# Two 64-wide heads per TensorE turn, or one: unpairing the half-array matmuls of two attention stages

## The reference

```python
def causal_mla_attention(q_nope, q_rope, k_nope, k_rope, v):   # 8 heads, q and k 64+32 wide, v 64 wide
    sc = einsum('bqhd,bkhd->bhqk', qn, k_nope) + einsum('bqhr,bkr->bhqk', qr, k_rope)
    sc = where(mask, sc * scale, -inf)
    p = softmax(sc, axis=-1)
    return einsum('bhqk,bkhd->bqhd', p, v)

def mixer_b(q, k, v, rel_bias):          # groups with (window, dilation) (128,1), (512,4), (2048,16)
    for g, (window, dilation) in enumerate(DIL_PAIRS):
        o, l = dilated_group(...)         # banded softmax with a bias by relative distance
    wts = softmax(stack(lses), axis=0)
    return sum(wts[..., None] * stack(outs), axis=0)
```

## Time and profile before

| | us |
|---|---|
| median of 3 runs | 1055.5 (1055.49 to 1056.89) |
| profiled execution | 1055.49 |
| its span in the trace | 1053.5 |
| TensorE busy | 1012.3 (96%) |
| VectorE busy | 700.0 (66%) |
| ScalarE busy | 536.9 (51%) |
| granted TensorE clock, mean | 0.993 |

### The profile page before, as it was taken

One profiled execution on the slowest core, in us unless ns is written; L12 is line 12 of the kernel. 1 busy time (PEld: TensorE's weight loads), 2 busy tenths in 40 slices (PEclk: granted clock), 3 DMA queues, 4 the chain that ended last, 5 costly groups with the idle time before them and its releaser, 6 DMA issues.

```text
span 1053.5 us, 19826 instructions
## 1 busy us (share of the span) xinstructions
PE 1012.3 (96%) x8502; PEld 983.1 (93%) x8502; DVE 700.0 (66%) x1213; ACT 536.9 (51%) x903; POOL 39.0 (4%) x75
## 2 busy tenths in 40 slices
PE   5999999999988999999999999999999999999995
PEld 3899999988987899999999999999999999999985
DVE  3478787556687577776756679655557765555485
ACT  4453444455555655544444477654455554445453
POOL 5000000010000001000000000004000000000000
PEclk8999999999999999999999999999999999999998
DMA  9979899875735346487573656436256575565511
GB/s 306 379 261 317 292 339 316 292 265 190 220 93 187 126 155 181 162 278 241 199 237 130 194 161 200 155 113 187 68 170 223 178 240 167 193 196 165 200 41 40
DMA packets 144463, 212.27 MB, mean 201 GB/s; under 512 B 4259, under 2 KB 121239, under 8 KB 144376
## 3 DMA queue, kind: packets, MB, share of 16 engines
q1 hardware_dynamic: 138928, 194.40, 55.6%
q0 software_dynamic: 5184, 16.30, 4.8%
q10 hardware_dynamic: 264, 0.31, 0.1%
HBM read 209.88 MB, written 1.11 MB: 200 GB/s over the span
## 4 chain that ended last, share of the span: by engine, by line
PE 63%; issue 22%; DVE 8%; DMA 3%; ACT 3%; SPq 0%; POOL 0%; POOLq 0%; DVEq 0%; ACTq 0%
PE PS L460 61%; DVE wlo L1774 4%; DMA SC<-in_w_ada_dram 3%; PE PS L468 1%; ACT whi L1291 1%; DVE SC L1732 1%; ACT SC L1278 1%; DVE xT L1741 0%; ACT SC L1283 0%; DVE SC L2207 0%; DVE W L1732 0%; DVE hl L1741 0%; DVE SC L1738 0%; DVE SC L1741 0%; DVE st L1744 0%
## 5 line engine op out<-in xcount | busy, mean ns | idle before, releaser
L1774 DVE TENSOR_TENSOR wlo<-raw,whi 128x1024 fp32r<-128x1024 f32 (+2 forms) x331 | 386.4, 1186 | 197.7 <-ACT whi L1291 197.3
L1291 ACT ACTIVATE whi<-raw 128x1024 fp32r<-128x1024 f32 (+2 forms) x331 | 331.5, 1022 | 173.9 <-PE PS L460 132.9
L460 PE MATMUL PS<-hh,whi 128*128 128x256 f32 (+1 forms) x1376 | 393.6, 286 | 8.0 <-DVE wlo L1774 5.8
L460 PE MATMUL PS<-hh,wlo 128*128 128x256 f32 (+1 forms) x1376 | 388.7, 282 | 0.0
L460 PE MATMUL PS<-hl,whi 128*128 128x256 f32 (+1 forms) x1376 | 387.8, 282 | 0.0
L460 PE MATMUL PS<-SR,whi 128*128 128x256 f32 (+1 forms) x1824 | 329.0, 283 | 3.9 <-DVE wlo L1774 1.4
L460 PEld LDWEIGHTS PS<-SR,whi 128*128 128x128 f32 x1824 | 279.8, 188 | 8.8 <-issue 3.1
L460 PEld LDWEIGHTS PS<-hh,whi 128*128 128x128 f32 x1376 | 260.3, 189 | 12.3 <-DVE wlo L1774 7.0
L460 PEld LDWEIGHTS PS<-hl,whi 128*128 128x128 f32 x1376 | 261.1, 190 | 0.4
L460 PEld LDWEIGHTS PS<-hh,wlo 128*128 128x128 f32 x1376 | 260.7, 189 | 0.0
L460 PE MATMUL PS<-SR,wlo 128*128 128x256 f32 (+1 forms) x912 | 256.6, 281 | 0.0
(11 more groups left out here) (183 smaller groups left out, 722.0 us busy)
## 6 DMA issues: line engine op xcount, KB each, us to landing
raw<-in_ffn_w_dram SPq DMA_DIRECT2D x60, 1024.0 KB, 7.2
raw<-in_w_in_dram SPq DMA_DIRECT2D x38, 1024.0 KB, 5.5
raw<-in_w_ff_dram SPq DMA_DIRECT2D x32, 1024.0 KB, 5.3
raw<-in_w_ada_dram SPq DMA_DIRECT2D x16, 1024.0 KB, 6.7
SC<-in_w_ada_dram POOLq DMA_DIRECT2D x12, 1024.0 KB, 5.7
SC<-in_w_ada_dram SPq DMA_DIRECT2D x8, 1024.0 KB, 12.3
raw<-in_w_out_dram SPq DMA_DIRECT2D x8, 1024.0 KB, 4.8
raw<-in_ffn_w_dram SPq DMA_DIRECT2D x8, 768.0 KB, 12.9
```

Source lines behind the costliest of these rows:

```text
L460: return e.matmul(o, l, r, start=start, stop=stop, skip_group_check=True)
L1291: e.activation(hi_part(p), raw_part(p), ACT.Copy).then_inc(*hi_done.up(p.i))
L1774: e.tensor_tensor(lo_part(p), raw_part(p), hi32(hi_part(p)), ALU.subtract).then_inc(*lo_done.up(p.i))
```

## The change

`values1`, `scores_b` and `values_b` take one head or unit at a time instead of two. The loops call them in every iteration: `values1(i - 3)` from i = 3, `scores_b(i)` for i below 8, `values_b(i - 2)` from i = 2. Each signals by itself, and each waits only for what it reads. In branch B the order of the units changes from (both heads of one T) to (both T of one head), and with it the addresses that the bias loads read; their sizes, number and buffers stay. The products are the same, and so is their number.

```diff
-            def values1(k):
-                b = (7, 3)[k % 2]
-                on.wait_ge(act_done, ("pt1", 2 * k), ("pt1", 2 * k + 1))
...
-                for j, (at, src) in enumerate(((0, slice(0, 256)), (128, slice(256, 384)))):
-                    for h in (2 * k, 2 * k + 1):
-                        po = 64 * (h % 2)
-                        m = mm(PS[po:po + 64, b, at:256], v_sb[:, j, 64 * h:64 * h + 64], pt1[h % 3][:, src], j == 0, j == 1)
-                m.then_inc(*count(("v1", 2 * k), ("v1", 2 * k + 1)))
+            def values1(h):
+                k, b = h // 2, (7, 3)[h // 2 % 2]
+                po, pt = 64 * (h % 2), pt1[h % 3]
+                on.wait_ge(act_done, ("pt1", h))
...
+                mm(PS[po:po + 64, b, 0:256], v_sb[:, 0, 64 * h:64 * h + 64], pt[:, 0:256], True, False)
+                mm(PS[po:po + 64, b, 128:256], v_sb[:, 1, 64 * h:64 * h + 64], pt[:, 256:384], False, True).then_inc(*count(("v1", h)))
...
-                if i >= 4 and i % 2 == 0:
-                    values1(i // 2 - 2)
+                if i >= 3:
+                    values1(i - 3)
...
-            def scores_b(n):
-                f0, T = n // 2, n % 2
-                on.wait_ge(*((act_done, ("s_a", 6), ("s_a", 7)) if n == 0 else (dve_done, ("s_b", 2 * n - 2), ("s_b", 2 * n - 1))))
...
-                    for half in range(2):
-                        at = slice(64 * half, 64 * half + 64)
-                        m = mm(PS[:, 4 + half, o:o + w], qbT[at, f, 128 * T:128 * T + 128], kbT[at, f, ks])
-                m.then_inc(*count(("s_b", 2 * n), ("s_b", 2 * n + 1)))
+            def scores_b(u):
+                s, T = u // 2, u % 2
+                b, po = 4 + u % 2, 64 * (s % 2)
+                on.wait_ge(*((act_done, ("s_a", 6 + u)) if u < 2 else (dve_done, ("s_b", u - 2))))
...
+                    m = mm(PS[:, b, o:o + n], qbT[po:po + 64, f, 128 * T:128 * T + 128], kbT[po:po + 64, f, ks])
+                m.then_inc(*count(("s_b", u)))
...
-            def values_b(n):
-                f, T = n // 2, n % 2
-                on.wait_ge(act_done, ("pt2", 8 + 2 * n), ("pt2", 9 + 2 * n), ("back2", 6), ("back2", 7), ("back2", 8))
...
-                for j in range(4):
-                    for half in range(2):
-                        s = 2 * f + half
...
-                m.then_inc(*count(("v_b", 2 * n), ("v_b", 2 * n + 1)))
+            def values_b(u):
+                s, T = u // 2, u % 2
+                po = 64 * (s % 2)
+                on.wait_ge(act_done, ("pt2", 8 + u), ("back2", 6), ("back2", 7), ("back2", 8))
...
+                for j, (blk, hd) in enumerate(((0, s), (1, s), (T, 4 + s), (T, 8 + s))):
+                    m = mm(PS[po:po + 64, 7, 128 * T:128 * T + 128], vb[:, blk, 64 * hd:64 * hd + 64], pt2[u % 2][:, 128 * j:128 * j + 128], j == 0, j == 3)
+                m.then_inc(*count(("v_b", u)))
 
             for i in range(10):
-                if i < 8 and i % 2 == 0:
-                    scores_b(i // 2)
+                if i < 8:
+                    scores_b(i)
                 behind2(1)
                 if 1 <= i <= 8:
                     turn2("b", i - 1, False)
-                if i >= 3 and i % 2:
-                    values_b((i - 3) // 2)
+                if i >= 2:
+                    values_b(i - 2)
...
             for u in range(8):
-                s, T, half = 2 * (u // 4) + u % 2, u // 2 % 2, u % 2
+                s, T = u // 2, u % 2
```

More of the change, by code:

```diff
@@ L798, in turn1 @@
                 m.then_inc(*count(("pt1", h)))
-            def values1(k):
-                b = (7, 3)[k % 2]
-                on.wait_ge(act_done, ("pt1", 2 * k), ("pt1", 2 * k + 1))
[L803 to L808, removed]
-                for j, (at, src) in enumerate(((0, slice(0, 256)), (128, slice(256, 384)))):
-                    for h in (2 * k, 2 * k + 1):
-                        po = 64 * (h % 2)
-                        m = mm(PS[po:po + 64, b, at:256], v_sb[:, j, 64 * h:64 * h + 64], pt1[h % 3][:, src], j == 0, j == 1)
-                m.then_inc(*count(("v1", 2 * k), ("v1", 2 * k + 1)))
+            def values1(h):
+                k, b = h // 2, (7, 3)[h // 2 % 2]
+                po, pt = 64 * (h % 2), pt1[h % 3]
+                on.wait_ge(act_done, ("pt1", h))
+                if h % 2 == 0:
+                    if k == 0:
+                        on.wait_ge(act_done, ("qkT", 1, 1))
+                    elif k == 1:
+                        on.wait_ge(*back1_free(6))
+                    else:
+                        on.wait_ge(dve_done, ("oa", k - 2))
+                mm(PS[po:po + 64, b, 0:256], v_sb[:, 0, 64 * h:64 * h + 64], pt[:, 0:256], True, False)
+                mm(PS[po:po + 64, b, 128:256], v_sb[:, 1, 64 * h:64 * h + 64], pt[:, 256:384], False, True).then_inc(*count(("v1", h)))
             for i in range(HEADS + 3):
@@ L1033, in pe_program @@
             behind2(2)
-            def scores_b(n):
-                f0, T = n // 2, n % 2
-                on.wait_ge(*((act_done, ("s_a", 6), ("s_a", 7)) if n == 0 else (dve_done, ("s_b", 2 * n - 2), ("s_b", 2 * n - 1))))
-                for g, (o, w) in enumerate(((0, 256), (256, 128), (384, 128))):
-                    f = 2 * g + f0
+            def scores_b(u):
+                s, T = u // 2, u % 2
+                b, po = 4 + u % 2, 64 * (s % 2)
+                on.wait_ge(*((act_done, ("s_a", 6 + u)) if u < 2 else (dve_done, ("s_b", u - 2))))
+                for g, (o, n) in enumerate(((0, 256), (256, 128), (384, 128))):
+                    f = 2 * g + s // 2
@@ L1040, in scores_b @@
                     on.wait_ge(dve_done, ("back2", f // 2), ("back2", 3 + f // 2))
                     ks = slice(0, 256) if g == 0 else slice(128 * T, 128 * T + 128)
-                    for half in range(2):
-                        at = slice(64 * half, 64 * half + 64)
-                        m = mm(PS[:, 4 + half, o:o + w], qbT[at, f, 128 * T:128 * T + 128], kbT[at, f, ks])
-                m.then_inc(*count(("s_b", 2 * n), ("s_b", 2 * n + 1)))
-            def values_b(n):
-                f, T = n // 2, n % 2
-                on.wait_ge(act_done, ("pt2", 8 + 2 * n), ("pt2", 9 + 2 * n), ("back2", 6), ("back2", 7), ("back2", 8))
-                if n == 0:
+                    m = mm(PS[:, b, o:o + n], qbT[po:po + 64, f, 128 * T:128 * T + 128], kbT[po:po + 64, f, ks])
@@ L1051, in values_b @@
+                m.then_inc(*count(("s_b", u)))
[3 more added lines that the diff above has]
+                on.wait_ge(act_done, ("pt2", 8 + u), ("back2", 6), ("back2", 7), ("back2", 8))
+                if u == 0:
                     on.wait_ge(dve_done, ("oA", 7))
-                if n == 2:
+                if u == 4:
                     on.wait_ge(dve_done, ("oB", 0))
-                for j in range(4):
-                    for half in range(2):
-                        s = 2 * f + half
-                        blk, hd = ((0, s), (1, s), (T, 4 + s), (T, 8 + s))[j]
-                        m = mm(PS[64 * half:64 * half + 64, 7, 128 * T:128 * T + 128], vb[:, blk, 64 * hd:64 * hd + 64],
-                               pt2[half][:, 128 * j:128 * j + 128], j == 0, j == 3)
@@ L1263, in pool_program @@
                     src = bass.AP(scratch.tensor, base, [[1, 128], [255, n], [1, 128]])
-                    e.dma_start(bias_at[half][:, o:o + 128 * n].rearrange("p (c k) -> p c k", k=128), src).then_inc(*bias_in[half].landed(u))
+                    e.dma_start(bias_at[T][:, o:o + 128 * n].rearrange("p (c k) -> p c k", k=128), src).then_inc(*bias_in[T].landed(u))
             on.wait_ge(dve_done, ("gm", 3, 7))
@@ L2393, in dve_program @@
                 if i < 8:
-                    c, half, p = st[:, 160 + 8 * (i % 4):168 + 8 * (i % 4)], i % 2, p2[(8 + i) % 3]
+                    c, T, p = st[:, 160 + 8 * (i % 4):168 + 8 * (i % 4)], i % 2, p2[(8 + i) % 3]
                     lo_for(("s_b", i))
-                    on.wait_ge(bias_in[half], i)
+                    on.wait_ge(bias_in[T], i)
                     on.wait_ge(mm_done, ("s_b", i), ("pt2", 5 + i))
@@ L2399, in dve_program @@
                         on.wait_ge(dve_done, ("p2", "b", i - 4))
-                    e.tensor_tensor_reduce(p, PS[:, 4 + i % 2, :], bias_at[half], -1.0, 3.0e38, ALU.add, ALU.min,
+                    e.tensor_tensor_reduce(p, PS[:, 4 + i % 2, :], bias_at[T], -1.0, 3.0e38, ALU.add, ALU.min,
                                            accum_out=c[:, 0:1]).then_inc(*dve_done.up(("s_b", i)))
```

## The result

| | before | after |
|---|---|---|
| median, us | 1055.95 (4 runs, 1055.49 to 1056.89) | 1066.16 (4 runs, 1064.69 to 1067.33) |
| profiled execution, its span, us | 1055.49, 1053.5 | 1066.5, 1064.5 |
| granted clock, mean | 0.993 | 0.989 |

The account below looks back on a forecast made before the run. TensorE was taken to bound branch B fully, and the first block only beyond its waits for VectorE and ScalarE. Branch B 7.8 plus first block 1.3 made 9.1 us on 1055.49: 1064.6 us, range 1061.0 to 1068.0.

Parts of the forecast that it names:

- A lone unit costs a pair's time: Attention groups: paired halves share one 0.109 us slot, so a lone unit takes as many slots as a pair.
- Rival A: Both stages: half an array takes half a slot, 0.055 us; only entries and exits cost, +1.2 us; chance 0.07.
- Rival C: Branch B: lone units show their weight loads, about +4 us more, 1068.8 us; chance 0.05.
- The number of new groups: Branch B: one scores group, three of values and scores, one of values are new, 9.4 us in sum.
- The wait of 1.6 us goes: End of branch B: fewer ScalarE pieces ahead of the last transposes' copy, so TensorE's 1.6 us wait ahead of last values disappears.
- Branch B +7.8: Branch B: new groups cost 9.4 us with nothing to hide them, less the 1.6 us wait.
- First block: First block's attention: four new `values1` groups, 4.0 us in all, partly taken up by three waits; 1.3 us remain.
- 0.81 in iteration 6, and 0.2 is left: First block's attention: the second new 1.0 us group meets a 0.81 us wait, leaving TensorE 0.2 us late.
- Rival B: Waits only move: first block pays all 4.0 us, branch B's 1.6 stays, 1068.9 us; chance 0.10 including half of it.
- Nothing vanishes behind the stages: Behind both attention stages: hardly a wait is left, so the whole 9.1 us delay reaches the end.
- The total: Whole kernel: 9.1 us on 1055.49 us gives 1064.6 us, 0.9% slower.
- the ends of these waits don't move: First block's attention: ScalarE and VectorE are the chain and keep their order, so TensorE's waits end when they did.

Follow-up runs that it names:

- e2: Only `scores_b` unpaired, units in the old order, against the kernel before; ratio 1.0058.
- e3: Only `values_b` unpaired, units in the old order, against the kernel before; ratio 1.0031.
- e5: Kernel before, pairs kept, with the last piece ahead of ScalarE's last `pt2` copy in branch B moved behind it; ratio 0.9994.
- e8: Kernel after, with the last piece put ahead of ScalarE's last `pt2` copy in branch B again; 1067.05 us in one execution.
- e6: e5, plus ScalarE doing its pieces one step earlier in the first block's attention; 1050.21 us, ratio 0.993 against the kernel before.
- e1: Only `values1` and its call unpaired, branch B as in the kernel before; ratio 1.0007, 1057.59 us.
- e10: e6 with the unpaired `values1` of after; ratio 0.9956 against the kernel before.
- e4: Kernel before, pairs in one group, but all matmuls of one half ahead of the other's in all three pair groups; ratio 1.0034.
- e9: Kernel before, `values_b` alone with halves alternating in blocks of three, three, one and one matmuls; 1058.22 us in one execution.
- e7: Kernel before, halves alternating in blocks of two matmuls in all three pair groups; 1057.97 us in one execution.

## Why the prediction was right

- **A lone unit costs a pair's time: right.** 8 records in 1.09 us, starts 0.11 us apart but for the first pause of 0.16, groups of 2.84 us for 2.86. Rival A needed gaps of 0.055 and is refuted. Rival C needed gaps of 0.14 to 0.19, and is refuted by the same rows. The Trainium skill (TensorE: Matmul & The Clock Gate, Part 3), from which C came, ties the overlap of weight loads to different row groups; the lone groups load the same tile record after record and hide loads of 0.136 and 0.186 us all the same, so the measurement decides against that rule here. The same part also lets a load run ahead into a background weight buffer; no run here shows whether that is what happens.
- **The number of new groups: right.** The parts are 5.0 + 3.1 us in e2 and e3, 7.57 in after.
- **The wait of 1.6 us goes because unit 6's key is noted one iteration earlier: right,** shown by e5 and e8 from both sides.
- **Branch B +7.8: right**, with 7.57. The wait that went was worth 1.7 (e5, e8) rather than the 1.6 shown.
- **First block: the mechanism was right, the size 0.3 too large.** 0.98 us for 1.3. The step that failed is "0.81 in iteration 6, and 0.2 is left" and the like: it set groups of 1.0 us against the waits as shown, and each wait is worth 0.16 more (e6). So iteration 4 takes 0.99 of 1.31 + 0.16 and leaves 0.48, shown as 0.33; iteration 6 takes 0.97 and leaves TensorE late by nothing, iteration 8 likewise with 1.03. Only the fourth group, 0.99, is left, and 0.98 was measured. e1 repeats it, and e10 shows four full prices without cover. Rival B, waits that only move, needed 4.0 and is refuted.
- **Nothing vanishes behind the stages: right**; up to 832 us 0.27 came on top, 0.16 of it a longer wait.
- **The total**: 8.8 us of the two traces are the change. Of the 9.1 forecast 0.3 is missing in the first block and 0.2 in branch B, and 0.3 came on top behind it. The median came out at 1066.16 rather than 1064.6 and in the profiled execution (1066.5) the rest is 2.2 us at the start and the end of the kernel, for which the forecast had nothing. The medians of before moved too, from 1055.95 to 1057.4 us in later sets of runs. That the other executions of after lost time in the same places was not seen, since they have no trace.

What the prediction hadn't seen: it took ScalarE's lateness in the first block as given ("the ends of these waits don't move"). It was a matter of ScalarE's order, worth 4.7 us of the stretch and 1.4 ahead of it (e6).

## What to carry to other kernels

In these groups two half-array float32 matmuls on different tiles cost one slot as long as they stand within four records of each other in TensorE's program; a lone one costs the same slot, so count slots and not matmuls before splitting a pair. Look for each new group whether a wait ends behind it: the same four groups cost 1.0 us where another engine was late and 3.9 where it wasn't. A wait of TensorE behind a column tile is worth what is shown and the overlap of two records (0.16 us) on top. And where TensorE waits for a short copy, look at what stands in front of the copy on its engine: moving the conversions by one step gained 6.1 us in a stage where the pairs are worth 3.9 at most.

## What was unexpected of the hardware

**Tiles overtake.** In e4 and e9 a record of the second half starts beside a record that stands four places ahead of it, so before three others of the first half. The Trainium skill (TensorE: Matmul & The Clock Gate, Part 2) says that matmuls stay in program order and only weight loads are pulled ahead; across tiles these traces differ from that.

**The granted clock near the end.** Near the end TensorE waits 2.0 us for `wlo`. From the start of the matmul ahead of this wait to the end of the last matmul, before, e3, e4, e6, e7 and e8 take 25.25 to 25.27 us, and after, e1, e2, e5, e9 and e10 take 26.75 to 26.82. TensorE around the wait and behind it, of before and of after (length, busy of PE; granted clock):

```profile
1015.50:1020.50 5.00, 3.02 (x26) 1.00 0.00 0
1020.50:1024.50 4.00, 4.00 (x36) 1.00 0.02 4
```

```profile
1025.00:1030.00 5.00, 3.02 (x27) 1.00 0.00 0
1030.00:1034.00 4.00, 4.00 (x23) 0.57 0.02 4
```

Both have the same 2.0 us of idle TensorE; behind it the clock stayed at the level of 2.4 GHz in the one and fell to mostly 1.2 GHz in the other, which costs 1.5 us. Kernels with and without the change are on both sides, so it isn't the change's. Together with the start (a wait for `wlo` ahead of the first block's attention ends between 305.5 and 308.2 us in the twelve traces), it is why the stages were compared and not the spans. What decides between the two was not tried.
